# The causal mask of the first attention: two identity matmuls on TensorE replaced by one add on VectorE

## The reference, cut to what matters

```python
def diff_attention(q, k, v, lam):
    ...
    def block(args):                      # one block of 128 queries, all heads
        qi, i = args
        s = jnp.einsum('bhcqd,bhckd->bhcqk', qi, kt).astype(jnp.float32)
        q_pos = i * Q_BLOCK + jnp.arange(Q_BLOCK)
        s = jnp.where(k_pos[None, :] <= q_pos[:, None], s, -jnp.inf)
        p = jax.nn.softmax(s, axis=-1)
        a = p[:, :, 0] - lam * p[:, :, 1]
        return jnp.einsum('bhqk,bhkv->bhqv', a.astype(vt.dtype), vt)
```

## Time and profile before

| | |
|---|---|
| median of 3 runs | 2017.31 us (2015.11 to 2018.63) |
| the profiled execution, its own time | 2014.95 us |
| its span, first to last instruction | 2013.2 us |
| mean granted clock of TensorE | 0.991 of full (2.4 GHz) |
| the differential attention | from about 26 us to about 320 us |
| one head in the hardware loop | about 32.1 us |

### The profile page before, as it was taken

How to read it: one execution, slowest core, us unless ns; L and a number is a source line. 1 busy time by engine, 2 the same in 40 slices (tenths; PEclk the granted TensorE clock), 3 DMA queues, 4 the chain that set the end, 5 groups by cost and what they waited for, 6 DMA issues and landing times.

```text
span 2013.2 us, 30871 instructions
## 1 busy us (share of the span) xinstructions
PE 1969.5 (98%) x11878; PEld 1692.0 (84%) x11878; DVE 1058.4 (53%) x1618; ACT 737.1 (37%) x1158; POOL 66.7 (3%) x112
## 2 busy tenths in 40 slices
PE   7999998999999999999999999999999999999998
PEld 6777776888887888888899999999999889999886
DVE  4666666666525355553354555555576364444433
ACT  4433333332223333232335455555553243233222
POOL 2000000000002000000110000000000020000000
PEclk8999998999999999999999999999999999999999
DMA  5222211222232333223232222222222323333321
GB/s 162 74 63 73 63 53 53 74 73 63 87 112 73 110 91 92 86 91 115 63 112 78 74 74 74 74 74 67 71 74 74 105 74 94 94 94 94 101 98 52
DMA packets 244001, 167.24 MB, mean 83 GB/s; under 512 B 5293, under 2 KB 231701, under 8 KB 243910
## 3 DMA queue, kind: packets, MB, share of 16 engines
q1 hardware_dynamic: 242224, 160.98, 27.0%
q10 hardware_dynamic: 1286, 4.23, 0.7%
q0 software_dynamic: 400, 0.72, 0.1%
HBM read 163.81 MB, written 2.10 MB: 82 GB/s over the span
## 4 chain that ended last, share of the span: by engine, by line
PE 79%; issue 18%; DVE 2%; ACT 1%; DMA 0%; POOL 0%; ACTq 0%; SPq 0%; POOLq 0%; DVEq 0%
PE pj L1658 9%; PE pj L1660 9%; PE pj L1659 9%; PE pj L1211 5%; PE pj L1212 5%; PE pj L1210 5%; PE zz L1211 2%; PE zz L1210 2%; PE zz L1212 2%; PE pj L1267 2%; PE pj L1268 2%; PE pj L1269 2%; PE zz L1267 2%; PE zz L1269 2%; PE zz L1268 2%
## 5 line engine op out<-in xcount | busy, mean ns | idle before, releaser
L1978 DVE TENSOR_TENSOR w_lo<-raw,w_hi 128x1024 fp32r<-128x1024 f32 x299 | 365.1, 1222 | 300.3 <-ACT w_hi L634 296.7
L634 ACT ACTIVATE w_hi<-raw 128x1024 fp32r<-128x1024 f32 x299 | 314.6, 1053 | 211.5 <-PE tr L1269 139.1
L1658 PE MATMUL pj<-x_hi,w_hi 128*128 128x258 f32 (+1 forms) x1280 | 367.2, 287 | 0.0
L1659 PE MATMUL pj<-x_lo,w_hi 128*128 128x258 f32 (+1 forms) x1280 | 361.5, 282 | 0.0
L1660 PE MATMUL pj<-x_hi,w_lo 128*128 128x258 f32 (+1 forms) x1280 | 361.5, 282 | 0.0
L1210 PE MATMUL pj<-x_hi,w_hi 128*128 128x512 f32 x760 | 308.5, 406 | 1.7 <-ACT gate L703 1.7
L1211 PE MATMUL pj<-x_lo,w_hi 128*128 128x512 f32 x760 | 303.0, 399 | 0.0
L1212 PE MATMUL pj<-x_hi,w_lo 128*128 128x512 f32 x760 | 300.7, 396 | 0.0
L1659 PEld LDWEIGHTS pj<-x_lo,w_hi 128*128 128x128 f32 x1280 | 241.9, 189 | 0.8
L1658 PEld LDWEIGHTS pj<-x_hi,w_hi 128*128 128x128 f32 x1280 | 241.5, 189 | 1.1
L1660 PEld LDWEIGHTS pj<-x_hi,w_lo 128*128 128x128 f32 x1280 | 241.9, 189 | 0.0
(11 more groups left out here) (576 smaller groups left out, 3501.4 us busy)
## 6 DMA issues: line engine op xcount, KB each, us to landing
raw<-in_l_w_in_dram SPq DMA_DIRECT2D x113, 512.0 KB, 4.0
raw<-in_w_in_dram SPq DMA_DIRECT2D x64, 512.0 KB, 4.0
raw<-in_w_up_gate_dram SPq DMA_DIRECT2D x44, 512.0 KB, 3.8
raw<-in_l_w_out_dram SPq DMA_DIRECT2D x32, 512.0 KB, 3.4
raw<-in_w_down_dram SPq DMA_DIRECT2D x22, 512.0 KB, 3.3
raw<-in_w_proj_conv_dram SPq DMA_DIRECT2D x8, 512.0 KB, 3.8
raw<-in_w_proj_attn_dram SPq DMA_DIRECT2D x8, 512.0 KB, 3.7
raw<-in_w_out_dram SPq DMA_DIRECT2D x8, 512.0 KB, 3.3
```

The costliest lines, as they stand in the source:

```text
L634: act.activation(w_hi[:, slot], raw[:, slot], ACT.Copy).then_inc(hi_done, 1)
L1658: pe.matmul(dst, w_hi[:, slot, k, :], hi[:, k, tok], start=(k == 0), stop=False)
L1659: pe.matmul(dst, w_hi[:, slot, k, :], lo[:, k, tok], start=False, stop=False)
L1978: dve.tensor_tensor(w_lo[:, slot], raw[:, slot], w_hi[:, slot].bitcast(F32), ALU.subtract).then_inc(lo_done, 1)
```

## The change

`scores` on PE loses the two matmuls with the mask, and the product of q and k becomes the first write of its bank (`start=True`). `maxima` on DVE gains one instruction, ahead of the maxima: it adds the mask to the diagonal blocks of both maps in place in PSUM (128 partitions x 2 x 128, the mask read twice), and the maxima wait for it through `link`. The count of link steps in the hardware loop goes from 4 to 5 for each of the four rounds.

```diff
@@ scores(hd, qt, par), PE
                 need(pe, DA["exp"], j * 2)
                 for c in range(2):
-                    pe.matmul(zz[:, c, qt * P:n], ident_b[:], mask_le[:], start=True, stop=True)
-                for c in range(2):
                     r = slice(c * QD, (c + 1) * QD)
-                    ins = pe.matmul(zz[:, c, 0:n], qT[r, par, qt * P:n], kT[r, par, 0:n], start=False, stop=True,
-                                    skip_group_check=True)
+                    ins = pe.matmul(zz[:, c, 0:n], qT[r, par, qt * P:n], kT[r, par, 0:n], start=True, stop=True)
                 ins.then_inc(DA["scores"], 1)
@@ maxima(hd, qt), DVE
                 dve.wait_ge(DA["scores"], j + 1)
+                diag = zz[:, :, qt * P:n]
+                link(dve.tensor_tensor(diag, diag, mask_le[:].unsqueeze(1).to_broadcast([P, 2, P]), ALU.add))
                 for c in range(2):
                     ins = dve.tensor_reduce(mx[:, c:c + 1], zz[:, c, 0:n], AX_X, ALU.max)
                 link(ins)
@@ the hardware loop over heads, DVE
-                link.loop(i, 2 * (4 * 4 + 1 + 2))
+                link.loop(i, 2 * (4 * 5 + 1 + 2))
```

## The result

The changed kernel takes 2028.57 us in the median of 5 runs (2026.9 to 2028.95); the kernel before 2017.62 us in 5 runs. The ratio is 1.0054, with a 95% interval of 1.004 to 1.0067: slower by 0.5%, some 11 us. The forecast was 2025.7 us with a range of 2019.5 to 2031.0.

A forecast was written before the change was run, and what follows sets the result against it. Each loop head was taken as bound by VectorE up to block 3's transposes, then by TensorE. Adds +6.9 us, mask pairs -1.9 us gave 2022.3 us; two clock falls, +3.4 us, gave 2025.7 us, range 2019.5 to 2031.

The forecast's parts named there:

- DVE's part: Loop head from the mean (142.29) to `pa` (159.17): VectorE has no slack of its own and sets the pace.
- the turn: PE's transposes of query block 3 in round 0, which wait 0.73 us until DVE has written `pa`.
- The price and the count of the add: DVE's mask add ahead of the maxima: 0.46 us each with link, 15 on the path, +6.9 us.
- the dearer estimate: DVE's add writing PSUM: by the skill's access overheads, some 2 us more, a sum of +7.0 us.
- The mask pair: PE's two mask matmuls ahead of the scores: 0.21 us per pair, nine pairs count, 1.9 us off.
- PE's part: Loop head from 159.30 to the next mean at 174.52: PE sets the pace, DVE idles 3.02 and 2.46 us.
- the other pairs: Mask matmuls of blocks 2, 3 and 0 in a loop head: removing them only lengthens PE's wait, worth nothing.
- The length of a head: Hardware loop after the change: 32.8 us where the clock holds, 34.5 us where it falls.
- The clock: After round 0's longer PE idle: falls in two of seven heads, 1.7 us each, +3.4 us; chance 0.54.
- The idle of PE: Round 0 after the change: PE idles 2.3 us in 2.8 us, around the scores.
- The first piece: PE's idle in round 0 before the scores, waiting for the exponentials: 0.98 us.
- The sum alone: Rival: adds minus mask pairs, granted clock stays at 1.00 in all heads: 2022.3 us; chance 0.28.

The follow-up runs named there:

- the last version: Kernel before with a 1.22 us weight step moved out of VectorE's stretch and VectorE masking blocks 0 and 1 only: 2009.98 us, ratio 0.9969.
- The filled gap: Changed kernel plus seven unused 512-column matmuls in TensorE's round 0 gap of each head from 2 on: 2022.54 us, ratio 1.0036.
- the change with the step moved: Changed kernel with the rest of round 3's weight tile, 1.22 us on VectorE, formed in the next head's round 0: 2015.95 us, ratio 0.9997.
- the version with the adds in the waits and the step moved: Changed kernel, adds of blocks 2 and 3 in VectorE's waits, 1.22 us weight step moved, head 0's block 3 mask on TensorE: 2012.25 us, ratio 0.9981.
- the version with the adds in the waits: Changed kernel with the adds of blocks 2 and 3 moved to where VectorE waits for GpSimd's power and ScalarE's rounding: 2017.06 us, ratio 1.0006.

## Why the prediction was right, point by point

**DVE's part sets the pace up to the turn: right.** The turn waits for `pa` in all heads, and the wait grew. Moving one step out of that part removed the wait and brought 31.41 us a head; doubling the adds in it brought 0.93 us a head.

**The price and the count of the add: right.** 0.426 us for the instruction and 0.46 us from start to start, as taken. Writing to PSUM in place cost no more than reading from it; the dearer estimate from what the Trainium skill, Perfetto Trace Analysis, section Optimizing Scalar/DVE Operations, gives for PSUM did not come true here. Two adds a head on the path, 0.94 us. In the tail from the turn of head 8 to that of head 9 it is 27.14 us against 26.21, another two; the clock was low there for 8 us against 5 us before, but without any mask the same stretch took 26.22 us with 8 us of low clock, so the difference is not the clock's.

**The mask pair: mis-sized.** Taken at 0.21 us, "since start to start is what the next instruction feels". It is worth 0.10 to 0.16 us, near the lower bound of 0.12 us: PE's part went from 14.24 us (159.30 to 173.54) to 14.08 us (162.86 to 176.94), and 0.26 us came from two pairs in the last version. With 0.15 us the sum is 15 x 0.46 - 9 x 0.15 = 5.6 us in place of 5.0. The filled gap gives 5.8 us by the medians, 7.3 us by the ratio (4.4 to 9.9).

**That the other pairs are worth nothing: right.** Without any mask at all a loop head is at most 0.16 us shorter.

**The length of a head: right.** Forecast 32.8 us with the clock held and 34.5 us with a fall; measured 32.85 and 32.87 us, and 34.40 to 34.64 us.

**The clock: right in kind, low in number.** Forecast were two falls at 1.7 us; the profiled execution has four at 1.5 to 1.8 us. The filled gap shows that they come from PE's idle and what they cost, 6.5 us over the six heads. The step that was low is the guess of two of seven: it was not worked out from rows, only placed between one gap that did nothing and one that did. The total still lies in the range because the range allowed up to five falls; had the guess been one, the mechanism would have been as right and the forecast further off. The other four timed runs have mean clocks of 0.985 to 0.987, so the profiled one is no exception. The Trainium skill, TensorE: Matmul & The Clock Gate, section HAM oscillation, says that a gap in each turn of a loop can throttle the clock in each turn; here it did so in four of seven.

**The idle of PE:** forecast 2.3 us, measured 1.85 to 2.03 us in heads 3 to 8. The first piece was 0.64 to 0.76 us and not 0.98: two pairs give PE 0.3 us and not 0.42, and the profile counts idle from the modelled end of the last matmul of the product, 0.16 us behind the point from which I counted.

The sum alone was forecast as 2022.3 us; the filled gap, in which no head has a fall, gives 2022.54 us. That the two agree so closely is in part luck: the filler kernel lost 1.9 us to the change behind the turn of head 8.

## What to carry to other kernels

Before moving work from a full engine to a half idle one, follow both engines around one turn of the loop and see in which part each step lies: 0.15 us taken from PE and 0.46 us given to DVE lose where DVE's part ends last and win where DVE waits. An edit that makes TensorE wait longer can cost twice, by the wait and by the clock behind it; look at the granted clock of each turn, not at the mean, and by stage, since falls elsewhere can move a total by as much as the edit. If a chain on the other engine sets the pace, first look for a step in it that nobody waits for: moving one such step brought 3.4 us here by the ratio (1.6 to 5.2), and no placement of the mask that was tried without it beat the kernel before.

## What the runs showed of the hardware that was not expected

Whether the clock falls does not hang on the length of the idle alone. With 0.7 and 1.1 to 1.3 us of idle and 0.49 us of matmuls between them it fell in four of six heads of the change (it held at 162.86 and at 299.22). With 1.56 and 1.30 us it held in head 2 of the change and fell in head 2 of the change with the step moved; with 0.97 and 1.30 us it fell in head 2 of the version with the adds in the waits and the step moved, and held in head 2 of the last version; with 1.94 and 1.30 us it held in head 2 of the version with the adds in the waits. With 2.8 to 3.0 us together, 3.3 us in head 2 (adds doubled on blocks 2 and 3), it fell in five of seven. Runs of one kernel scatter as well: the version of the waits had runs from 2014.88 to 2020.66 us, with mean clocks from 0.987 to 0.993. That the moment of the gap decides would fit, but no run varied the moment alone.
